# A float32r decoder step on one Trainium2 core: rows of the high input at a pitch of 1296 bytes, and 16 bytes between weight buffers

## What is computed

```python
h = rms_norm(x, p['g_pre_mix'])
z = jnp.einsum('btd,de->bte', h, p['w_in'])          # 2048 -> 16464
...
x = x + rms_norm(jnp.einsum('bte,ed->btd', u, p['w_out']), p['g_post_mix'])
h = rms_norm(x, p['g_pre_x'])
x = x + rms_norm(cross_attend(h, p['w_xq'], mem_k, mem_v, p['w_xo']), p['g_post_x'])
h = rms_norm(x, p['g_pre_ffn'])
y, new_buf = conv_ffn(h, conv_buf, p['w_up'], p['conv_w'], p['conv_b'], p['w_down'])
x = x + rms_norm(y, p['g_post_ffn'])
```

## Time and profile before

| | |
|---|---|
| median of 3 runs | 2733.12 us (2731.53 to 2734.34) |
| span of the profiled execution | 2732.5 us |
| TensorE busy (PE) | 2686.0 us, 98% |
| VectorE busy (DVE) | 1602.1 us, 59% |
| ScalarE busy (ACT) | 1075.3 us, 39% |
| GpSimd busy (POOL) | 207.7 us, 8% |
| mean busy share of the 16 DMA engines for the slabs' queue | 53.8% |

### The profile page before, as it was taken

One profiled execution on the slowest core, in us unless ns is written; L12 is line 12 of the kernel. 1 busy time (PEld: TensorE's weight loads), 2 busy tenths in 40 slices (PEclk: granted clock), 3 DMA queues, 4 the chain that ended last, 5 costly groups with the idle time before them and its releaser, 6 DMA issues.

```text
span 2732.5 us, 49450 instructions
## 1 busy us (share of the span) xinstructions
PE 2686.0 (98%) x20118; PEld 2555.5 (94%) x20118; DVE 1602.1 (59%) x2383; ACT 1075.3 (39%) x1357; POOL 207.7 (8%) x295
## 2 busy tenths in 40 slices
PE   8999999999999999999999999999999999999998
PEld 7999887899999999999989969999999999999997
DVE  5564564476777767777546334485655555653334
ACT  5333445444444444444333234342332233343324
POOL 0102311111111111111100000000000000000000
PEclk9999999999999999999999999999999999999999
DMA  9746656765555556555464694555555555555554
GB/s 268 206 124 164 214 169 209 225 192 157 155 141 159 154 149 163 141 159 154 132 200 130 223 385 110 144 167 149 154 146 146 153 150 144 142 139 150 153 151 146
DMA packets 693464, 458.69 MB, mean 168 GB/s; under 512 B 13646, under 2 KB 661422, under 8 KB 687342
## 3 DMA queue, kind: packets, MB, share of 16 engines
q1 hardware_dynamic: 681008, 414.25, 53.8%
q0 software_dynamic: 8608, 28.06, 3.6%
q10 hardware_dynamic: 3712, 14.35, 1.4%
HBM read 429.91 MB, written 26.72 MB: 167 GB/s over the span
## 4 chain that ended last, share of the span: by engine, by line
PE 93%; DVE 3%; DMA 2%; ACT 1%; issue 0%; SPq 0%; POOL 0%; DVEq 0%; ACTq 0%
PE psum L596 20%; PE psum L601 20%; PE psum L598 20%; PE psum L852 4%; PE psum L1284 4%; PE psum L1285 4%; PE psum L1286 4%; PE psum L857 2%; PE psum L994 1%; PE psum L997 1%; PE psum L990 1%; DMA ring<-in_w_in 1%; PE psum L1165 1%; PE psum L710 1%; PE psum L1006 1%; PE psum L1044 1%
## 5 line engine op out<-in xcount | busy, mean ns | idle before, releaser
L596 PE MATMUL psum<-x_high,w_high 128*128 128x320 f32 x3808 | 1123.8, 311 | 0.5 <-ACT w_high L2022 0.5
L598 PE MATMUL psum<-h_low,w_high 128*128 128x320 f32 x3312 | 974.3, 309 | 0.0
L1331 DVE TENSOR_TENSOR w_low<-ring,w_high 128x2048 fp32r<-128x2048 f32 x292 | 676.1, 2315 | 312.8 <-ACT w_high L2022 312.4
L2022 ACT ACTIVATE w_high<-ring 128x2048 fp32r<-128x2048 f32 x294 | 561.6, 1911 | 678.2 <-PE psum L601 554.9
L596 PEld LDWEIGHTS psum<-x_high,w_high 128*128 128x128 f32 x3808 | 713.0, 188 | 5.8 <-issue 2.4
L598 PEld LDWEIGHTS psum<-h_low,w_high 128*128 128x128 f32 x3312 | 621.9, 188 | 1.6
L601 PE MATMUL psum<-x_high,w_low 128*128 128x320 f32 x3808 | 597.4, 309 | 0.0
L601 PEld LDWEIGHTS psum<-x_high,w_low 128*128 128x128 f32 x3808 | 568.5, 188 | 0.0
L1284 PE MATMUL psum<-y_high,w_down_high 128*128 128x320 f32 x704 | 217.8, 309 | 1.2 <-DVE w_low L1941 1.2
L1286 PE MATMUL psum<-y_high,w_low 128*128 128x320 f32 x704 | 216.3, 307 | 0.0
L1285 PE MATMUL psum<-y_low,w_down_high 128*128 128x320 f32 x704 | 216.2, 307 | 0.0
(11 more groups left out here) (424 smaller groups left out, 2840.9 us busy)
## 6 DMA issues: line engine op xcount, KB each, us to landing
ring<-in_w_in SPq DMA_DIRECT2D x128, 1024.0 KB, 5.8
ring<-in_w_up SPq DMA_DIRECT2D x88, 1024.0 KB, 5.8
ring<-in_w_down SPq DMA_DIRECT2D x64, 704.0 KB, 4.8
ring<-in_w_xk SPq DMA_DIRECT2D x16, 1024.0 KB, 5.7
ring<-in_w_xv SPq DMA_DIRECT2D x16, 1024.0 KB, 5.0
ring<-in_w_out SPq DMA_DIRECT2D x16, 1024.0 KB, 6.0
ring<-in_w_xq SPq DMA_DIRECT2D x16, 1024.0 KB, 6.2
ring<-in_w_xo SPq DMA_DIRECT2D x16, 1024.0 KB, 6.0
```

Of the source, the lines that this page charges most:

```text
L596: mm(out, w_hi[:, j % 2, k, :], x_hi[:, k, :], start=k == 0, stop=False)
L598: mm(out, w_hi[:, j % 2, k, :], lo[:, k, :], start=False, stop=False)
L1331: V.tensor_tensor(w_lo[:, j], ring[:, j], w_hi[:, j % 2].bitcast(FP32), ALU.subtract).then_inc(N.slab_lo, 1)
L2022: F(w_hi[:, j % 2], ring[:, j], ACT.Copy).then_inc(N.slab_hi, 1)
```

## The change

It changes places in memory only. PAD is 4 elements, 16 bytes. Rows of x_high get a pitch of 324 elements (1296 bytes) of which 320 are used; the two buffers of w_high and the four slots of the ring (and so w_low) get a pitch of 2052 elements, of which 2048 are used. The constants give up 96 columns of a place that other buffers reuse ("room"), to make room for it. m_high now ends where w_high begins, as x_high does.

By the built program x_high then starts at 192096, w_high at 212832, ring at 16512 and h_low at 49344. The phases of x_high's rows are 32, 48, 0, 16 and so on in turn, those of w_high's buffers 32 and 48, those of w_low's slots 0, 16, 32, 48. h_low, w_down_high and y_high's quarters 1 to 3 stay at 0; zq_low, m_low, y_low and y_high's quarter 0 stay at 32; m_high goes from 0 to 32.

The instructions of each engine are the same ones in the same order. ScalarE's and GpSimd's copies into four rows of x_high, and the two transfers of x_high, now name 4 (or 16) rows of 320 elements where they named one run; the transfer of the constants is 96 columns narrower.

```diff
@@ -47,7 +47,10 @@
-ARENA = 53184 - R * KD * P - KD * T
+PAD = 4
+XP = T + PAD
+WP = KD * P + PAD
+ARENA = 53184 - R * WP - KD * T
@@ -75,7 +78,7 @@
-for _name, _cols in (("ident", 128), ("ones", 128), ("level", 6 * 32), ("blocks", 128), ("room", 960), ("causal", 512),
+for _name, _cols in (("ident", 128), ("ones", 128), ("level", 6 * 32), ("blocks", 128), ("room", 864), ("causal", 512),
@@ -162,8 +165,9 @@
-        ring = ctx.enter_context(nc.sbuf_tensor("ring", [P, R, KD, P], FP32))[:]
-        h_at = ring_at + 4 * R * KD * P
+        ring = ctx.enter_context(nc.sbuf_tensor("ring", [P, R, WP], FP32))[:]
+        ring = ring[:, :, 0:KD * P].rearrange("p r (k n) -> p r k n", n=P)
+        h_at = ring_at + 4 * R * WP
@@ -191,11 +195,12 @@
-        w_lo = alias("w_low", ring_at, R, KD, P)
-
-        SPLIT_AT = ARENA - KD * T - 2 * KD * P
-        x_hi = alias("x_high", arena_at + 4 * SPLIT_AT, KD, T)
-        w_hi = alias("w_high", arena_at + 4 * (SPLIT_AT + KD * T), 2, KD, P)
+        w_lo = alias("w_low", ring_at, R, WP)[:, :, 0:KD * P].rearrange("p r (k n) -> p r k n", n=P)
+
+        SPLIT_AT = ARENA - KD * XP - 2 * WP
+        x_hi = alias("x_high", arena_at + 4 * SPLIT_AT, KD, XP)[:, :, 0:T]
+        W_AT = SPLIT_AT + KD * XP
+        w_hi = alias("w_high", arena_at + 4 * W_AT, 2, WP)[:, :, 0:KD * P].rearrange("p r (k n) -> p r k n", n=P)
@@ -277,7 +282,7 @@
-        M_HI = SPLIT_AT + KD * (T - MEM)
+        M_HI = W_AT - KD * MEM
...
```

More of the change, by code:

```diff
@@ L354, in hybrid_layer @@
         assert top[0] <= MIX + KD * T
-        kx_slot.append(arena[:, SPLIT_AT + KD * T:SPLIT_AT + KD * T + 2 * D].rearrange("p (m d) -> p m d", m=2))
+        kx_slot.append(arena[:, W_AT:W_AT + 2 * D].rearrange("p (m d) -> p m d", m=2))
         top[0] = SPLIT_AT
@@ L359, in hybrid_layer @@
         ppT = take(2, 2 * SEQ)
-        assert top[0] <= SPLIT_AT + KD * T
+        assert top[0] <= W_AT
         top[0] = BASE
```

## The result

| | before | after |
|---|---|---|
| median | 2734.4 us (15 runs, 2731.5 to 2736.6) | 2739.3 us (15 runs, 2736.0 to 2742.1) |
| ratio | | 1.0017, 95% interval 1.0009 to 1.0025 |
| span of the profiled execution | 2732.5 us | 2735.5 us |

The forecast was 2720. The kernel after is 4.9 us slower. That is inside the 0.2% that the forecast calls the same, but clear of the noise, as the interval leaves out 1; 13 us faster was forecast.

What follows compares the result with a forecast made beforehand. TensorE, busy 98%, bounds the kernel: number of matmuls times spacing. Mixed places gave -13 us, all other terms 0: span 2732.5 to 2719.5, with the runs' median 0.6 above, 2720 us; range 2664 to 2757.

Steps and rivals of the forecast that it cites:

- Conversions: Copies into x_high and subtraction for h_low walk gapped rows: at most 2 us, under 1 on the path; taken as 0.
- Slabs: Weight loads of 1 MB into slots at multiples of 16 bytes: landing in 5.8 us, cover 14 us; taken as 0.
- x_high's return: x_high brought back in four pieces with shorter lines: first piece's landing could cost +0 to +2 us; taken as 0.
- rival (d): Slab transfers to 16-byte places land late, over 14 us; at 1 us for each of 294 slabs, 3027; chance 0.01.
- the price of mixed places: 12,560 matmuls, mostly 320 columns: mixed phases gain 1.0 ns each, as in the down projection's quarters, -13 us.
- the 2112 matmuls of the down projection left where they are: Down projection, only w_low's slots moved: no change counted; with 768 of the memory projection, 3 us either way at 1 ns.
- the forecast's own signs of a wrong mechanism: L601's spacing stays while time moves, or spacing moves by the same amount in parts whose phases didn't change.
- surplus taken for collisions: The 13.4 ns over a 320-column matmul's columns look like moving columns colliding with weight loads; up to 10.3 ns could go, -129 us.
- rival (a): Phases 16 and 48 remove half or more of the surplus: 65 us, 2668; all of it, 2604; chance 0.14.
- (c): Nothing: surplus is weight handover without regard to addresses, or mixed phases average to where it was; 2733; chance 0.17.
- (b): Slower: steps between x_high's rows and to h_low cost time; 1 ns per matmul gives 2746, +2.9 ns 2769; chance 0.32.
- The rule that speaks against it: Trainium skill: TensorE's two independent read ports never wait on anyone, so placement is worth nothing; time stays at 2733.

Runs made afterwards that it cites:

- micro4: Bare TensorE matmuls without the layer: one loop after 16 predecessors, and patterns with one operand moved on; same loop 146.7 or 144.4 ns.
- x_only: Kernel before with only x_high's row pitch of 1296 bytes, w_high's and w_low's places modulo 64 kept: 2741.8 us, ratio 1.0027.
- no_ring: Kernel after without the 16 bytes between the ring's slots, x_high's and w_high's gaps kept: 2738.9 us, ratio 1.0016 against before.
- micro1: Layer left out, 31 loops of bare matmuls varying places, pitches, weight columns, moving columns and types: 146.7 ns for 320 float32r columns with operands at 0.
- h80: Kernel before with the low input moved 80 bytes on; high input, high weights and ring unmoved: 2718.2 us, ratio 0.9948.
- w48_main: Kernel before with w_low's ring and w_high 48 bytes on, pitches as before: 2741.2 us, ratio 1.0028.
- w48_all: Kernel before with w_low's ring, w_high and w_down_high at 48 modulo 64, zq_low and y at 0: 2741.7 us, ratio 1.0029.
- h176w80: Kernel before with buffers moved so that, from the high input, low input is at 176, high weights 80, low weights 96 modulo 256: 2718.7 us, ratio 0.9948.
- k80: Kernel before with three buffers moved: from the high input, low input at 80, low weights at 48, high weights at 0 modulo 256: 2723.5 us, ratio 0.9959.
- micro2: Layer left out, bare matmuls: 272 to 352 moving columns, and the up pattern at 64 places modulo 64: means 144.1 to 147.3 ns.
- micro5: The map modulo 256: bare matmuls, low input and high weights at 16 places each, low weights random: settled pairs 143.3 to 150.0 ns.

## Why the prediction was wrong, point by point

**Right: what bounds the kernel.** The time is the number of matmuls times their spacing. Waits of TensorE were to stay near 40 us and are 42.0, that for x_high's first piece under 3 and is 2.2; instructions are the same; L710 stayed.

**Right: the side terms.** Conversions 0: busy times of VectorE and ScalarE moved by 0.6 and 0.2 us. Slabs 0: they land in 5.8 us as before. x_high's return 0 to 2 us: 1.3 us, where I took the lower end. Nothing of rival (d).

**Wrong: the price of mixed places.** The step that failed is "the nearest row is the down projection ... 1.0 ns, times 12,560 = -13 us". Measured in the up projection, the pairs moved by +0.2 ns and the singles by -0.4, a slab by -0.1 ns a matmul. The row was sound but its reason was not: I put the 1.0 ns down to places modulo 64, mixed against equal, and carried it over to any mixture. micro4 moved the same quarters from 145.6 to 147.5 with all places modulo 64 kept. The gain belonged to one combination of places modulo 256, and another mixture need not inherit it. The map shows what a place drawn at random brings on average: 146.71 ns, which is nothing. That the kernel's own mixture stays close to that mean is measured; why it does is open, as the map misses x_only and no_ring by 0.9 and 0.5 ns.

**Wrong: the 2112 matmuls of the down projection left where they are.** I allowed 3 us either way and took 0; they lost 2.1 us. The quarters should have changed "with their slot alone": they didn't. Quarter 0 went from 146.4 to 148.8 ns though its slot is the one of before; its inputs stand 320 bytes lower, the high weights 64 higher, which modulo 64 is nothing. A spacing that moves where no phase did is close to one of the forecast's own signs of a wrong mechanism.

**Wrong: surplus taken for collisions.** The reading of L710 (no surplus at half the pace) suggested that up to 10.3 ns could go, and made room for rival (a). Its 272.8 ns are also misread: 14.73 us for 54 contain a first distance of 373 ns and the last one's latency of 433. The steady distance is 269 ns, which would have made the bound 12 ns. micro1 shows 13.3 ns with the same operands each time and with a quarter of the weight columns. The lowest mean in any map is 143.3 ns: of the 13.3 ns, places can move 3.4 down and 3.3 up. What the other 10 ns are stays open.

**The rivals.** (c), nothing, came closest: the time is 4.9 us above before, and the slabs stayed within 0.1 ns. What fits is its second reason, that the mixture averages to where it was. Its first, that the surplus has nothing to do with addresses, is wrong. (b) named the down side rightly in kind, steps between rows, but its price of 1 ns was found only in parts: singles of no_ring +0.7, the down projection +1.1. (a) is out as told, yet its sign was to be had: h80 gained 0.5% by a place, not by a mixture.

**The rule that speaks against it.** By the measured rows, TensorE's spacing of the same instructions runs from 143.3 to 150.0 ns by the places of its operands, with no other engine at work. The Trainium skill, "SBUF — State Buffer", section "Who interferes with whom", has it never wait on anyone, in a passage on SBUF's ports. Its spacing in bare matmuls is that of the kernels within 0.4 ns, so beside waits for data no run here shows another engine in its way; but its own two streams aren't free of each other's places, or of something else that addresses decide.

## What to carry to other kernels

Before spacing buffers out, ask whether the new places are a chosen combination or a random draw: a draw costs and brings nothing on average (146.71 against 146.67 ns here), though a single one cost up to 0.3% (x_only, w48_main, w48_all), and a chosen one brought 0.5% for 80 bytes. A map with bare matmuls at the kernel's own pitches, over places modulo 256 and in whole slabs so that transients are in it, foretold the pairs of h80 and h176w80 within 0.1 ns in slabs that follow each other. It did not foretell that in h80 32 of 47 slabs behind other matmuls gain nothing; a map meant for a kernel should hold what stands before its slabs as well. A map modulo 64 misled, and for k80 one of settled loops promised twice the gain. And a difference of 1 ns between two parts of a trace is evidence on these two parts, until its cause is known.

## What the runs showed of the hardware

- float32r matmuls with all operands at 0 follow each other at their columns over 2.4 GHz plus 13.3 ns (120.0, 146.7, 173.3 and 226.7 ns for 256, 320, 384 and 512; micro1), whether 32 or 128 weight columns are loaded; at other lengths the surplus was 11.7 to 16.7 ns (micro1, micro2). Bfloat16 had 2.5 ns (135.8 for 320). A plain float32 product is two instructions of 269.1 ns each.
- The spacing depends on the places of the operands to each other: over the 256 combinations modulo 256 bytes 143.3 to 150.0 ns in pairs, 146.7 in 161 of them (micro5). For the high input in pairs the period is 256 bytes, not less (micro4).
- The same loop over the same operands settles in one of several repeating cycles of starts (144.4 or 146.7 ns in micro4, 143.3 or 146.7 in h80's slabs), and what ran before picks which. What state carries this over, and why places act at all, no run here shows.
- A change of pattern costs a transient: the pairs at 80, 0, 48 have 143.3 ns settled and 144.8 in slabs of 16 pairs.
